# Four experts of 32 rows side by side in TensorE's column groups, with unsplit fp32 weights, expert by expert

## What is computed

```python
def expert_block(args):                    # xb: rows of one expert
    xb, e = args
    hdn = jax.nn.silu(xb @ w1[e]) * (xb @ w3[e])    # w1, w3: 1024 x 512
    return hdn @ w2[e]                              # w2: 512 x 1024
...
return jnp.zeros((t, d), xn.dtype).at[row_tok].add(ys * row_w[:, None])
```

## Time and profile before

| | |
|---|---|
| runs | 2045.43 us median of 3 (2041.5 to 2047.73) |
| span of the profiled execution (the page gives no other time of it) | 2040.7 us |
| TensorE busy / weight load | 1934.7 us (95%) / 1661.2 us (81%) |
| VectorE, ScalarE busy | 1381.1 us (68%), 1164.5 us (57%) |
| DMA | 418.32 MB, mean 205 GB/s |
| the experts of the first block | about 254 to 797 us of the span |

### The profile page before, as it was taken

The page is one execution under the profiler, slowest core; times in us unless marked ns, Lnnn a source line. Parts: engine busy times, 40 slices in busy tenths (PEclk is TensorE's granted clock), DMA queues, the critical chain, the costliest instruction groups (busy, mean ns, idle before and its releaser), DMA issues. The chain is left out here.

```text
span 2040.7 us, 29427 instructions
## 1 busy us (share of the span) xinstructions
PE 1934.7 (95%) x11449; PEld 1661.2 (81%) x11449; DVE 1381.1 (68%) x1837; ACT 1164.5 (57%) x1850; POOL 5.5 (0%) x25
## 2 busy tenths in 40 slices
PE   7999799999999998999898999998999999999997
PEld 6988488888888885489765869998999998888886
DVE  3672489999999996326342336998888885666665
ACT  3452289999999995334242324443577764455444
POOL 1000000000000000000000000000000000000000
PEclk9999799999999999899699989998999999999999
DMA  8433289999999997334113013554543345555553
GB/s 329 166 124 127 93 326 396 382 378 371 375 376 381 376 399 255 136 124 165 62 42 124 10 53 102 184 183 147 182 135 135 133 137 185 196 191 192 195 195 135
DMA packets 84960, 418.32 MB, mean 205 GB/s; under 512 B 14091, under 2 KB 16592, under 8 KB 51930
## 3 DMA queue, kind: packets, MB, share of 16 engines
q1 hardware_dynamic: 74592, 406.98, 54.1%
q10 hardware_dynamic: 10234, 9.48, 1.6%
HBM read 415.36 MB, written 1.06 MB: 204 GB/s over the span
## 5 line engine op out<-in xcount | busy, mean ns | idle before, releaser
L2150 DVE TENSOR_TENSOR slot_lo<-arena,w_hi 128x2048 fp32r<-128x2048 f32 x192 | 433.6, 2286 | 23.9 <-ACT w_hi L1590 22.5
L2508 DVE TENSOR_TENSOR tab_lo<-arena,tab_hi 128x1024 fp32r<-128x1024 f32 x256 | 312.3, 1224 | 122.9 <-ACT tab_hi L1929 120.9
L1590 ACT CAST w_hi<-arena 128x2048 fp32r<-128x2048 f32 x192 | 363.1, 1916 | 6.8 <-PE bank L1047 6.7
L1929 ACT CAST tab_hi<-arena 128x1024 fp32r<-128x1024 f32 x256 | 267.6, 1046 | 0.2
L1473 PE MATMUL bank<-x_hi,tab_lo 128*128 128x256 f32 x1024 | 144.9, 285 | 7.9 <-DVE tab_lo L2508 7.9
L1963 ACT CAST e_hi<-arena 128x256 fp32r<-128x256 f32 x128 | 52.0, 407 | 174.9 <-PE bank L1506 174.2
L1473 PE MATMUL bank<-x_hi,tab_hi 128*128 128x256 f32 x1024 | 148.4, 288 | 2.0 <-ACT tab_hi L1929 2.0
L1043 PE MATMUL bank<-w_hi,gathP 128*128 128x512 f32 x512 | 138.7, 393 | 5.4 <-ACT gathP L1611 5.4
L1936 ACT ACTIVATE arena<-bank 128x256 f32<-128x256 f32 (+16 forms) x128 | 43.8, 342 | 175.3 <-PE bank L1473 175.3
L1473 PE MATMUL bank<-nT_lo,tab_hi 128*128 128x256 f32 x1024 | 143.0, 281 | 0.0
L1506 PE MATMUL bank<-tab_hi,e_hi 128*128 128x512 f32 x512 | 137.6, 391 | 1.8 <-DVE arena L2547 1.8
(11 more groups left out here) (402 smaller groups left out, 3203.4 us busy)
## 6 DMA issues: line engine op xcount, KB each, us to landing
arena<-in_w_dram SPq DMA_DIRECT2D x192, 1024.0 KB, 7.5
arena<-in_peer_down_dram SPq DMA_DIRECT2D x128, 512.0 KB, 3.3
arena<-in_peer_up_dram SPq DMA_DIRECT2D x128, 512.0 KB, 3.3
arena<-in_packed_later_dram SPq DMA_DIRECT2D x36, 1024.0 KB, 7.1
arena<-in_packed_first_dram SPq DMA_DIRECT2D x28, 1024.0 KB, 7.3
arena<-in_packed_later_dram SPq DMA_DIRECT2D x2, 816.0 KB, 11.3
arena<-in_packed_later_dram SPq DMA_DIRECT2D x2, 768.0 KB, 8.5
h<-in_x_dram ACTq DMA_DIRECT2D x1, 1024.0 KB, 5.4
```

Source lines behind the costliest of these rows:

```text
L1590: nc.scalar.copy(hi_of(e, g), portion_of(slot, e, g)).then_inc(S("w_hi"), 1)
L1929: nc.scalar.copy(tab_hi[n % HI][:, :], tab[n % PR]).then_inc(S("table_hi"), 1)
L2150: nc.vector.tensor_tensor(portion_of(slot_lo, e, g), portion_of(slot, e, g), hi_of(e, g).bitcast(F32), ALU.subtract).then_inc(S("w_lo"), 1)
L2508: nc.vector.tensor_tensor(tab_lo[n % PR][:, :], tab[n % PR], tab_hi[n % HI][:, :].bitcast(F32), ALU.subtract).then_inc(S("table_lo"), 1)
```

## The change

`SLOTS` becomes 32. Four experts (`BATCH`) are worked together: their rows take 4 x 32 partitions of a PSUM bank, expert e of a batch partitions 32e to 32e+31. A batch has six steps (two for w1, two for w3, two for w2); a step is 16 calls of an unsplit fp32 product, stationary 128x32 (the rows), moving 128x512 (a quarter of a 1 MB piece), in the order expert 0 four times, expert 1 four times, and so on. The casts and the subtractions of the weights are gone, and so are `fold_halves`, `hid_hi` and `hid_lo`; `turn_hidden` transposes the two halves after the steps. A ring half is now freed four at a time, by step (`moe_steps`). SP's loop is written out. `pick` now holds all four groups of eight experts, so that none is overwritten; the gather makes 8 experts x 32 rows at once.

```diff
-SLOTS = 64
+SLOTS = 32
+STEPS = 6
+PICKS = 2 * BATCH * SLOTS
-            def portion(e, g, dst, stationary):
-                pe.wait_ge(S("w_hi"), turn_of[e, g] + 1)
-                for k in range(4):
-                    nc.tensor.matmul(dst, lhsT=stationary(k), rhs=hi_of(e, g)[:, k, :],
-                                     start=k == 0 and g in (0, 2, 4, 5), stop=False)
-                wait_lo(pe, e, g)
-                for k in range(4):
-                    mm = nc.tensor.matmul(dst, lhsT=stationary(k), rhs=portion_of(slot_lo, e, g)[:, k, :], start=False,
-                                          stop=k == 3 and g in (1, 3, 4, 5))
-                mm.then_inc(S("w13_used" if g < 4 else "w2_used"), 1)
+            def expert_step(b, step):
+                dst = bank[3 if step in (2, 3, 5) else 2]
+                if b and step in (0, 2):
+                    pe.wait_ge(S("out_lo"), 2 * b - 1 + step // 2)
+                if step == 0 and b % 2 == 0:
+                    pe.wait_ge(S("gath_read"), 2 * b + 4)
+                if step == 4:
+                    pe.wait_ge(S("hid_ready"), b + 1)
+                for e in range(BATCH):
+                    half_ready(pe, *moe_unit(b, step, e))
+                    for k in range(4):
+                        if step < 4:
+                            at = SLOTS * (BATCH * (b % 2) + e)
+                            lhsT = gathered[:, b // 2 % 2, 4 * (step % 2) + k, at:at + SLOTS]
+                        else:
+                            lhsT = hid[:, P * k + SLOTS * e:P * k + SLOTS * e + SLOTS]
+                        mm = nc.tensor.matmul(dst[SLOTS * e:SLOTS * e + SLOTS, :], lhsT=lhsT,
+                                              rhs=moe_weights(step, e)[:, k, :], start=k == 0 and step in (0, 2, 4, 5),
+                                              stop=k == 3 and step in (1, 3, 4, 5))
+                mm.then_inc(S("moe_steps"), 1)
...
+            def turn_hidden(b, v, out, ready, turned):
+                pe.wait_ge(S("turned_pick"), b + 1)
+                pe.wait_ge(S(ready), b + 1)
+                for f in range(FT):
+                    mm = nc.tensor.transpose(out[:, P * f:P * f + P], v[:, P * f:P * f + P], ident[:, :])
+                mm.then_inc(S(turned), 1)
...
+                for b in range(BATCHES):
+                    expert_step(b, 0)
+                    turn_pick(b)
+                    expert_step(b, 1)
+                    expert_step(b, 2)
+                    turn_hidden(b, a1, turn_bank, "a1_ready", "a1_turned")
+                    expert_step(b, 3)
+                    if b:
+                        for half in range(2):
+                            scatter(b - 1, half)
+                    turn_hidden(b, a3, more_bank, "a3_ready", "a3_turned")
+                    expert_step(b, 4)
+                    if b // 2 + 1 < BATCHES // 2:
+                        for x in range(2):
+                            gather(b // 2 + 1, 2 * (b % 2) + x)
+                    expert_step(b, 5)
...
-                nc.scalar.copy(hi_of(e, g), portion_of(slot, e, g)).then_inc(S("w_hi"), 1)
...
-                nc.vector.tensor_tensor(portion_of(slot_lo, e, g), portion_of(slot, e, g), hi_of(e, g).bitcast(F32),
-                                        ALU.subtract).then_inc(S("w_lo"), 1)
...
+            def hid_product(b):
+                dve.wait_ge(S("silu_ready"), b + 1)
+                dve.wait_ge(S("a3_turned"), b + 1)
+                nc.vector.tensor_tensor(hid, hid, bank[1][:, :], ALU.mult).then_inc(S("hid_ready"), 1)
...
+            for b in range(BATCHES):
+                for step in range(STEPS):
+                    src = w[("w1", "w3", "w2")[step // 2]]
+                    for e in range(BATCH):
+                        n, x = moe_unit(b, step, e)
+                        if n - RING in spent_at:
+                            sp.wait_ge(S("tile_done"), spent_at[n - RING])
+                        else:
+                            sp.wait_ge(S("moe_steps"), STEPS * b + step - 2)
```

More of the change, by code:

```diff
@@ L294, in build, with pick_of @@
         gain_row = scratch(B0 + 4096, D)
[L296 to L325, removed]
+        def pick_of(b, t):
+            return pick[:, b // 2, t, P * (b % 2):P * (b % 2) + P]
         p_tok = scratch(M0 + 2560, TT, 256)
@@ L1025, in _, with gather @@
             phases["routed"] = phases["pe"]
-            def gather(g, k):
+            turn_bank, more_bank = bank[0], bank[1]
+            def gather(g, pair):
                 pe.wait_ge(S("pick_ready"), g + 1)
                 if g:
[L1033 to L1037, removed]
-                mm.then_inc(S("gathered"), 1)
@@ L1051, in hidden @@
[L1051 to L1077, removed]
+                    pe.wait_ge(S("silu_ready"), 2 * g - 1)
+                elif pair >= 2:
+                    pe.wait_ge(S("gath_read"), pair - 1)
+                b = more_bank if pair % 2 else turn_bank
+                for x in range(2):
+                    for n, xp in enumerate((xn_hi, xn_lo)):
+                        for t in range(TT):
+                            k = 2 * pair + x
+                            mm = nc.tensor.matmul(b[:, T * x:T * x + T], lhsT=xp[:, t, P * k:P * k + P],
+                                                  rhs=pick[:, g, t, :], start=n == 0 and t == 0,
+                                                  stop=n == 1 and t == TT - 1)
@@ new lines, in turn_pick @@
+            def turn_pick(b):
+                pe.wait_ge(S("gath_read"), 4 * (b // 2 + 1) if b % 2 == 0 else min(4 * (b // 2 + 1) + 2, 2 * BATCHES))
+                for t in range(TT):
+                    nc.tensor.transpose(turn_bank[:, P * t:P * t + P], pick_of(b, t).bitcast(F32), ident[:, :])
+                for t in range(TT):
+                    mm = nc.tensor.matmul(more_bank[:, 0:BATCH], lhsT=pick_of(b, t).bitcast(F32),
+                                          rhs=gatew[:, t, BATCH * b:BATCH * b + BATCH], start=t == 0, stop=t == TT - 1)
+                mm.then_inc(S("pick_turned"), 1)
@@ L1093, in _ @@
             over = pe.value_load(overfull[0:1, 0:1], min_val=0, max_val=1)
             with pe.If(over < 1):
[L1095 to L1115, removed]
@@ new lines, in _, with gather_out, pick_out @@
+            turn_bank, more_bank = bank[0], bank[1]
+            def gather_out(g, pair):
+                act.wait_ge(S("gathered"), 4 * g + pair + 1)
+                nc.scalar.copy(gathered[:, g % 2, 2 * pair:2 * pair + 2, :].rearrange("p k n -> p (k n)"),
+                               (more_bank if pair % 2 else turn_bank)[:, :]).then_inc(S("gath_read"), 1)
+            def pick_out(b):
+                act.wait_ge(S("pick_turned"), b + 1)
+                nc.scalar.copy(pickT[:, b % 2, :, :].rearrange("p t s -> p (t s)"), turn_bank[:, 0:2 * P])
+                for e in range(BATCH):
+                    rows = slice(SLOTS * e, SLOTS * e + SLOTS)
+                    ins = nc.scalar.copy(row_w[rows, b % 2:b % 2 + 1], more_bank[rows, e:e + 1])
+                ins.then_inc(S("turned_pick"), 1)
@@ L2196, in _ @@
+            with dve.If(over < 1):
+                for g in range(1, BATCHES // 2):
+                    one_hots(g)
+                for b in range(BATCHES):
+                    hid_product(b)
+                    for half in range(2):
+                        rows_lo(b, half)
+                dve.wait_ge(S("scattered"), 2 * BATCHES)
                 for c in range(4):
```

336 lines of the change are left out of this document (110 added, 226 removed).

## The result

The changed kernel takes 1981.9 us (median; 1977.4 to 1982.6) against 2043.5 us: ratio 0.969, 95% interval 0.967 to 0.971, 62 us faster. The forecast said 2156 us and slower. In the profiles the span goes from 2040.7 to 1975.0 us, and all of it lies in the experts: their last scatter ends at 729.2 instead of 796.2 us. What follows is shifted and takes 1.3 us longer.

The account below looks back on a forecast made before the run. The prediction took TensorE to bound the experts: start 261.4, products 591.3, other work 49.5, drains 4 and last record 0.4 put their end at 906.6 us, +110 us, so 2156 us in all, range 2130 to 2255.

Parts of the forecast that it names:

- What bounds the kernel now: Experts' stretch before the change: TensorE sets the rate, 16.7 us an expert; transfers could do 2.47 us a piece.
- What an unsplit product costs: Expert products: a 128x512 fp32 call is two records of 0.43 us, 0.86 us, not shortened by 32 stationary columns.
- the case of no sharing: Expert steps: column groups never overlap, 1536 records at 0.43 us, 2225 us; chance 0.24, with or without bare loads.
- What the order lets run at once: Expert steps: only an expert's eighth record overlaps the next expert's first; 29 slots a step, 1375 slots, 591.3 us.
- rival 2: Expert steps: each column group has its own queue, 8 slots a step, transfers bound; 1964 us, chance 0.08.
- the strict queue: TensorE's calls: one in-order queue; only one call's last record and the next's first overlap, in different array parts.
- The other work on TensorE's path: Between expert steps: gather, turns, scatter, the wait for `hid` (8.2 us) and the end, unhidden, 49.5 us in all.
- a drain of 4: Some 40 changes between full-width and 32-column products may each cost a drain: 0 to 7.6 us, taken as 4.
- What costs nothing: Experts' stretch: ended casts and subtractions, remaining copies and the ring's transfers add no time; DMA share about 0.75.
- the free groups: Expert steps: four experts work at once whatever the order, 3.4 us a step, transfers bound; 1964 us, chance 0.08.
- the rival of the low clock: Expert products: 32 stationary columns keep TensorE at 1.2 GHz, 0.86 us a record; 2772 us, chance 0.06.
- the two cases with little or no sharing: Expert steps: 29 slots each, 2156 us (0.53), or no overlap of column groups, 2225 or 2251 us (0.24).

Follow-up runs that it names:

- before_q: The kernel before the change with a quarter of each expert transfer, cast and subtraction still at full size: 2046.2 us, ratio 1.0001.
- same_q: The changed kernel with a quarter of each transfer and all four experts in one column group, as one accumulation: 2227.8 us.
- expert_q: The changed kernel with only a quarter of each transfer, every product reading that quarter, order kept: 1957.2 us.
- round_q: The changed kernel with a quarter of each transfer and the experts taking turns, one product each: 1730.9 us.
- pairs_q: The changed kernel with a quarter of each transfer and the experts taking turns, two products each: 1735.6 us.
- round_full: The changed kernel with full transfers and the experts taking turns, one product each: 1974.7 us, ratio 0.966 to the kernel before.

## Why the prediction was wrong, step by step

**What bounds the kernel now**: right. before_q rules out the transfers, and the waits speak for TensorE against the engines that prepare its operands. Right too was the reading that the transfers could do 2.47 us a piece (2.49 measured over 450 us).

**What an unsplit product costs**: right. 0.43 us a record, 32 columns or 128; same_q came to 2227.8 us where the case of no sharing had been put at 2225.

**What the order lets run at once**: this is the step that failed. The forecast said that of an expert's eight records "only the eighth shares its slot with the next expert's first", 29 slots a step and 1375 in all. The runs show four of eight shared, 20 slots alone and 36 for two steps: 904 by expert_q, a difference of some 470 slots or 202 us, more than the whole miss. The evidence could not carry the claim. L1276 alternates between two parts of the array, so between its ends its records come by twos under either queue; the prediction said so itself under rival 2, and then used "by twos and never more" as the argument for the strict queue. A pattern with two groups cannot show whether a third would have started. It could show something else, though, and there rival 2 was wrong that the pairs would look the same with free queues or a strict one. At its ends they would not: the strict queue as described starts the first record alone and ends with a single one, 17 slots for the 32 records. The trace of the kernel before has two starting together at the first end and two at the last (time slice, TensorE's busy time with the records in flight, the loads', clock, DMA):

```profile
984.62:984.64 0.02, 0.01 (x2) 0.01 (x2) 0.50 0.00 0
991.56:991.58 0.02, 0.02 (x2) 0.00 (x0) 1.00 0.00 0
991.58:991.60 0.02, 0.02 (x4) 0.00 (x0) 1.00 0.00 0
```

If two records that start together lie in different halves, as the prediction took it, the second call's first record had passed the first call's second.

**The other work on TensorE's path**: 49.5 us and a drain of 4. TensorE's idle time for `hid` was 6.8 and its loads' 8.7 against 8.2. The drains were not seen one by one, and no run shows what one costs. The sum was near: in same_q, where the records can't overlap, 260.7 us (its first expert product) to 975.4 us less 1536 x 0.429 us leaves 55.7, against 49.5 + 4 + 0.4 = 53.9.

**What costs nothing**: "the DMA share falls to about 0.75" was wrong as a consequence: steps of 8.6 us alone and 7.7 in pairs instead of 12.5 are below the 9.9 us that the prediction had named as the point where the cover is gone, and the transfers bound, at a share of 1.01. That switch had been put in the right place: a batch needs 55.9 us of TensorE and 59.6 of transfers.

**The rivals**: the one that came closest was the free groups, which had been given 0.08 and 1964 us. Its mechanism, transfers as the new bound, is what happened; that each group goes its own way whatever the order is not, but four places are enough to fall under 9.9 us a step. Its number is near by that bound and not by its picture of the groups. Of the 18 us between 1964 and 1982, 14 lie in the experts: the first step took 8.9 us rather than 3.4, so SP sent again at 268.5 and not 265 (3.5 us); a piece took 2.49 and not 2.47 (180 x 0.02 = 4 us); the last piece was there 6 us after the sum of the pieces; and from there to the last scatter it took 6.4 and not 5. The rest is 1.3 us behind the experts and a median that lies 6.9 and not 4.7 above the profiled span. The rule of the Trainium skill, TensorEngine Tiling, Key Properties, that different tiles can execute loads and matmuls in parallel, held: in round_q a lone step takes 3.64 us and in same_q 13.92, so four matmuls ran at once. It is silent on the order, and the order decides here (8.86 us in expert_q). The rule of the Trainium skill, TensorE: Matmul & The Clock Gate, Part 3, that a load overlaps with matmuls in flight only for another row group, did not hold here: all experts use all rows, and 1536 loads of 0.11 us stood beside the products (round_q would otherwise not reach 8 slots a step). The granted clock stayed at 1.00 in the stretches of the changed kernel, so the rival of the low clock didn't come true.

**The chances**: 0.77 on the two cases with little or no sharing rested on one row with another kind of group. With no row of the resource itself, the cases should have shared the chance more evenly.

## What to carry to other kernels

Column groups of TensorE work at the same time if the calls of one group in a row are few: with four groups and moving operands of 128x512, up to two plain fp32 calls (four records) in a row cost nothing, and of longer runs everything beyond four records blocks the next group. Where a change takes work off the bounding engine, first compute the next bound (here 9.9 us a step of transfers) and then ask only whether the new pace falls below it; the exact pace beyond that is worth nothing, as some 240 us of free TensorE time bought 7. Waits alone don't tell that bound: here they came to 3.6 us, and the steady 421 GB/s gave it away. And a stretch bound by transfers is shortened by starting them earlier: four pieces moved into an idle stretch brought 10 us.

## What the runs showed of the hardware

- Four column groups stream four different fp32 operands of 128x512 at once, each at 0.429 us a record, with no loss: 384 slots for 1536 records.
- A column group takes four records, the one that runs and three behind it, before it holds up the other groups (20 and 36 slots with runs of 8, 52 with runs of 16; pairs_q equals round_q within 1.8 us), and each group has its own places (four experts start together in pairs_q at 306.27). So records of different groups leave the program's order: at 531.19 in the changed kernel the second expert's first starts with the first expert's fifth, ahead of three that stand before it.
- 16 DMA engines moved 421 GB/s for 450 us on end with pieces of 1 MB, while TensorE worked on the pieces that had landed.
- TensorE's busy share was 49 of 50 us in the kernel before, in the changed one and in expert_q, at paces of 16.7, 14.9 and 13.8 us an expert: records that overlap fill the row, and the share doesn't tell the pace.
- In round_full, where TensorE stood waiting for transfers more than once in a step, the granted clock fell to 0.93 in the stretch shown, so that it stood at the lower of its levels for part of it; the transfers kept 421 GB/s there and set the pace, so no cost of it shows.
